# Per-token factors of the RWKV branch made in the projection instead of the chunk loop

## What is computed

```python
z = h @ lp['w_in'][:, :STATE_COLS]
zr = _centred_shift(z[..., 2 * RET_WIDTH:], lp['rwkv_mu'][:, :SHIFT_STATE_COLS])
k, v, wd, ad = _split(zr, (RWKV_WIDTH, RWKV_WIDTH, DECAY_LORA, ICLR_LORA))
kk = kk * lax.rsqrt(jnp.sum(kk * kk, axis=-1, keepdims=True) + 1e-12)
u = lp['rwkv_w0'][:, None, None, :] + jnp.einsum('btr,drc->dbtc', jnp.tanh(wd), lp['rwkv_w2'])
w = jnp.exp(-jnp.exp(-jax.nn.softplus(-u.astype(jnp.float32)) - 0.5))
a = jax.nn.sigmoid(lp['rwkv_a0'][:, None, None, :] + jnp.einsum('btr,drc->dbtc', ad, lp['rwkv_a2']))
k_dir = k[None] * (1.0 + (a - 1.0) * lp['rwkv_k_a'])
# per head and direction, token by token
sa = jnp.einsum('bhvk,bhk->bhv', s, -kkt)
s = (s * wt[:, :, None, :] + sa[..., None] * (kkt * at)[:, :, None, :]
     + vt[..., None] * kt[:, :, None, :])
y = jnp.einsum('bhvk,bhk->bhv', s, xt[5])
bonus = jnp.sum(qu['r'][None] * st['k'] * r_k, axis=-1, keepdims=True).sum(0) * st['v']
```

## Time and profile before

| | us |
|---|---|
| median of the runs | 4059.08 |
| runs | 4056.05, 4059.08, 4069.73 |
| the profiled execution's own time | 4071.43 |
| its span | 4069.6 |
| projection | 0 to about 1184 |
| chunk stage | about 1184 to 2181 |
| TensorE busy over the span | 3694.0 (91%) |
| VectorE, ScalarE, GpSimd busy | 2247.2, 1892.5, 671.5 |

### The profile page before, as it was taken

The page is one execution under the profiler, slowest core; times in us unless marked ns, Lnnn a source line. Parts: engine busy times, 40 slices in busy tenths (PEclk is TensorE's granted clock), DMA queues, the critical chain, the costliest instruction groups (busy, mean ns, idle before and its releaser), DMA issues. The chain is left out here.

```text
span 4069.6 us, 94464 instructions
## 1 busy us (share of the span) xinstructions
PE 3694.0 (91%) x39914; PEld 3087.6 (76%) x39914; DVE 2247.2 (55%) x3650; ACT 1892.5 (47%) x3029; POOL 671.5 (16%) x637
## 2 busy tenths in 40 slices
PE   7999999999978888888887978996699999999993
PEld 6878878888867777777776867785588888888883
DVE  5532533434337777777776865555444544454545
ACT  5533534433336666666565443332244444444443
POOL 1000000000012222222220333200011111111111
PEclk9999999999989999999999989998799999999997
DMA  7655565555442223322324366655366666666667
GB/s 260 199 188 183 179 198 155 154 157 158 149 145 73 69 78 81 81 79 74 96 65 124 111 221 225 202 168 189 134 206 217 214 217 212 214 206 214 212 212 299
DMA packets 378746, 673.49 MB, mean 165 GB/s; under 512 B 90428, under 2 KB 261540, under 8 KB 360712
## 3 DMA queue, kind: packets, MB, share of 16 engines
q1 hardware_dynamic: 351368, 580.69, 44.0%
q0 software_dynamic: 27008, 87.46, 7.4%
HBM read 524.89 MB, written 143.15 MB: 164 GB/s over the span
## 5 line engine op out<-in xcount | busy, mean ns | idle before, releaser
L113 PE MATMUL fro__acc<-fro__hT_hi,fro__wh 128*128 128x512 f32 (+1 forms) x1608 | 624.9, 389 | 11.8 <-DVE fro__hT_lo L2695 8.9
L114 PE MATMUL fro__acc<-fro__hT_hi,fro__wl 128*128 128x512 f32 (+1 forms) x1608 | 612.9, 381 | 0.0
L115 PE MATMUL fro__acc<-fro__hT_lo,fro__wh 128*128 128x512 f32 (+1 forms) x1608 | 612.8, 381 | 0.0
L2112 DVE TENSOR_TENSOR fin__wl<-fin__raw,fin__wh 128x4096 fp32r<-128x4096 f32 x96 | 424.7, 4424 | 316.8 <-ACT fin__wh L2056 316.8
L2701 DVE TENSOR_TENSOR fro__wl<-prj__w,fro__wh 128x1024 fp32r<-128x1024 f32 x201 | 246.3, 1225 | 637.6 <-ACT fro__wh L2484 637.6
L2056 ACT ACTIVATE fin__wh<-fin__raw 128x4096 fp32r<-128x4096 f32 x96 | 348.4, 3629 | 190.8 <-PE exp__acc L115 190.3
L113 PE MATMUL exp__acc<-fin__wh,exp__xh 128*128 128x512 f32 x1024 | 399.9, 390 | 0.8 <-DVE exp__xl L2117 0.8
L115 PE MATMUL exp__acc<-fin__wl,exp__xh 128*128 128x512 f32 x1024 | 398.5, 389 | 0.0
L114 PE MATMUL exp__acc<-fin__wh,exp__xl 128*128 128x512 f32 x1024 | 398.4, 389 | 0.0
L113 PEld LDWEIGHTS fro__acc<-fro__hT_hi,fro__wh 128*128 128x128 f32 x1608 | 303.7, 189 | 77.7 <-issue 22.2
L114 PEld LDWEIGHTS fro__acc<-fro__hT_hi,fro__wl 128*128 128x128 f32 x1608 | 303.8, 189 | 59.1 <-issue 3.6
(11 more groups left out here) (462 smaller groups left out, 7570.1 us busy)
## 6 DMA issues: line engine op xcount, KB each, us to landing
fin__raw<-in_w_x SPq DMA_DIRECT2D x96, 2048.0 KB
prj__w<-in_w_z SPq DMA_DIRECT2D x201, 512.0 KB, 4.1
s_zT<-fro__pool SPq DMA_DIRECT2D x128, 256.0 KB, 4.5
fro__wm<-in_w_mod POOLq DMA_DIRECT2D x16, 1024.0 KB, 5.8
mix__gate<-s_zT SPq DMA_DIRECT2D x64, 256.0 KB, 4.2
prj__xin<-in_tokens SPq DMA_DIRECT2D x18, 512.0 KB, 5.7
rwc__kS<-s_kS SPq DMA_DIRECT2D x36, 256.0 KB, 3.1
rwc__kkn<-s_kkn SPq DMA_DIRECT2D x36, 256.0 KB, 3.3
```

Of the source, the lines that this page charges most:

```text
L113: pe.matmul(out, sh, mh, start=first, stop=False)
L114: pe.matmul(out, sl, mh, start=False, stop=False)
L115: return pe.matmul(out, sh, ml, start=False, stop=last)
L2112: ve.tensor_tensor(wl[s][:, :, :], raw[s][:, :, :], wh[s][:, :, :], ALU.subtract).then_inc(w_lo, 1)
```

## The change

The low-rank products and everything that follows from them per token move from the chunk stage into the projection.

- **Projection.** For each key tile TensorE makes the decay products at five steps after the tile and the rate products at six (`low_rank`: two directions, high part over 128 rows, low part over 64), and in the last block, whose tiles are 513 tokens wide, a group of one-column products at seven. They use `rc` too. ScalarE applies the sigmoids with a bias (`rates`), VectorE makes kd, bb and the bonus product (`unit`) and the low parts (`rests`), GpSimd's queue stores sg, kd, bb and bon for both directions. Its transfers in the projection go from 165 to 317. kS, kka, rrk and waS are no longer written. `zo` has three buffers instead of four. The tiles stand in another order: wa first, keys and queries in pairs.
- **Chunk stage.** Decays, learning, both sigmoids, key1, key2, removal and the bonus product are gone. A load brings sg, bb, kd, kkn, rS and vS, each in three pieces with the upper half swapped, and bon whole: 19 transfers. There are three buffers for them instead of two, and the load for slab h+3 waits, among others, for the bonus matmul of slab h. beta and kappa are one operation each over 128 partitions. The small sums of carried decays go from VectorE to GpSimd.

The diff, cut to its core:

```diff
+    C, HC, NG, GH, LEV, B, LB = P, 64, 2, 4, 5, 4, 3
...
             def load(j):
-                d, c = j % 2, slab_at(j)
-                sp.dma_start(wS[d][0:64, :], T["waS"][0:64, ds(c, C)]).then_inc(lws[d], 16)
-                sp.dma_start(aS[d][0:64, :], T["waS"][64:128, ds(c, C)]).then_inc(lws[d], 16)
-                if j == 0:
-                    low_rank(0)
-                    low_rank_rows(0)
-                    sp.dma_start(scanm[:, :, :], T["scanm"]).then_inc(scan_in, 16)
-                for n in names:
-                    rows = T[n][:, ds(c, C)].rearrange("(q p) t -> p q t", p=P)
-                    if n != "vS":
-                        sp.dma_start(ld[d][n][:, :, :], rows).then_inc(lds[d], 16)
+                u, c = j % LB, slab_at(j)
+                for n in each_way + both_ways:
+                    rows = (T[n][j % 2] if n in each_way else T[n])[:, ds(c, C)].rearrange("(q p) t -> p q t", p=P)
+                    landed = lsg[u] if n == "sg" else lds[u]
+                    if n == "bon":
+                        sp.dma_start(ld[u][n][:, :, :], rows).then_inc(landed, 16)
                         continue
-                    sp.dma_start(ld[d][n][0:HC, :, :], rows[0:HC, :, :]).then_inc(lds[d], 16)
+                    sp.dma_start(ld[u][n][0:HC, :, :], rows[0:HC, :, :]).then_inc(landed, 16)
                     for s in range(2):
-                        sp.dma_start(ld[d][n][HC:P, :, side(s)], rows[HC:P, :, side(1 - s)]).then_inc(lds[d], 16)
+                        sp.dma_start(ld[u][n][HC:P, :, side(s)], rows[HC:P, :, side(1 - s)]).then_inc(landed, 16)
...
             for h in range(SLABS + 3):
-                if h + 2 < SLABS:
-                    for n in ("am", "kd1", "kd2", "bd", "al", "rho", "bonp", "trm"):
+                if h + LB < SLABS:
+                    for n in ("dd2", "betad", "kappad", "al", "rho", "trm", "bonm"):
                         sp.wait_ge(S[n], at(n, h))
-                    load(h + 2)
+                    load(h + LB)
...
+            def carried(j):
+                d = j % 2
+                gp.wait_ge(S["dd"], at("dd", j))
...
+                ways = []
+                for e in range(2):
+                    upto, after = halves(L)[side(e), :, :, 31], halves(D)[side(e), :, :, HC - 1]
+                    enter, leave = (upto, after) if d == 0 else (after, upto)
+                    s, o = turn_of(j, 0) ^ e, turn_of(j, 1) ^ e
+                    gp.tensor_tensor(fl[side(e), 0, :], enter[:, :, s], dl[d][side(e), :], ALU.add)
+                    last = gp.tensor_tensor(fl[side(e), 1, :], enter[:, :, o], leave[:, :, s], ALU.add)
+                    ways.append(leave[:, :, o])
+                last.then_inc(S["fld"], 1)
+                gp.wait_ge(S["fld"], at("fld", j))
+                for e in range(2):
+                    last = gp.tensor_copy(dl[d][side(e), :], ways[e])
+                last.then_inc(S["dld"], 1)
...
+            def scaled_removal(j):
+                ve.wait_ge(lds[j % LB], 16 * NLD * (j // LB + 1) + START)
                 ve.wait_ge(S["ebk"], at("ebk", j))
-                ve.wait_ge(S["bd"], at("bd", j))
                 if j:
                     ve.wait_ge(S["trm"], at("trm", j - 1))
-                tt(beta[0:HC, :, :], bb[0:HC, :, :], e_bk[0:HC, :, :], ALU.mult)
-
-            def scaled(j):
-                ve.wait_ge(S["kd2"], at("kd2", j))
-                for out, rows, signal in ((beta, bb, "betad"), (kappa, kd, "kappad")):
-                    if out is kappa:
-                        tt(out[0:HC, :, :], rows[0:HC, :, :], e_bk[0:HC, :, :], ALU.mult)
-                    for s in range(2):
-                        ins = tt(out[HC:P, :, side(s)], rows[HC:P, :, side(1 - s)], e_bk[HC:P, :, side(1 - s)], ALU.mult)
-                    ins.then_inc(S[signal], 1)
+                tt(beta[:, :, :], ld[j % LB]["bb"][:, :, :], e_bk[:, :, :], ALU.mult).then_inc(S["betad"], 1)
+
+            def scaled_keys(j):
+                tt(kappa[:, :, :], ld[j % LB]["kd"][:, :, :], e_bk[:, :, :], ALU.mult).then_inc(S["kappad"], 1)
...
                     levels(1, h)
                 if prepare:
                     exclusive(n)
-                if prepare:
-                    key1(n)
-                    removal(n)
                 if inverting:
                     levels(2, h)
-                if prepare:
-                    key2(n)
                 if exists(h - 2) and exists(h):
                     state(h - 2, 1)
                 if prepare:
-                    scaled_lower(n)
+                    scaled_removal(n)
                 if inverting:
                     levels(3, h)
                 if prepare:
-                    scaled(n)
-                    carried(n)
...
+            def rates(t, kind):
+                c, p = keys_of[t], ORDER[t][3]
+                j0, end, at = span(t)
+                m = min(end - j0, 512)
+                act.wait_ge(summed, use_of[t, kind] + 1)
+                for x in ((0, 1) if kind == "t" else (int(kind == "a"),)):
+                    out, stored = (sg, av)[x], (sg_out, bb_out)[x]
+                    for d in range(2):
+                        if kind == "t":
+                            ins = act.activation(out[d][:, 512:513], rc[:, x, d:d + 1], ACT.Sigmoid, bias=low_b[:, x, d, p:p + 1])
+                            continue
+                        if c:
+                            act.wait_ge(stored[d], 16 * c)
+                        ins = act.activation(out[d][:, 0:m], rc[:, d, 0:m], ACT.Sigmoid, bias=low_b[:, x, d, p:p + 1])
+                ins.then_inc(read, 1)
...
+            def low_rank(t, kind):
+                p = ORDER[t][3]
+                j0, end, at = span(t)
+                m = min(even(end - j0), 512)
+                pe.wait_ge(low_ok, 3)
+                pe.wait_ge(rank_in, 32 * (ORDER[t][0] + 1))
+                pe.wait_ge(read, use_of[t, kind])
+                for x in ((0, 1) if kind == "t" else (int(kind == "a"),)):
+                    own = slice(64 * x, 64 * x + 64)
+                    for d in range(2):
+                        hi, lo, mov = low_hi[:, x, d, p * P:(p + 1) * P], low_lo[own, d, p * P:(p + 1) * P], rank[x]
+                        if kind == "t":
+                            out = rc[:, x, d:d + 1]
+                            pe.matmul(out, hi.bitcast(F32), mov[:, 512:513].bitcast(F32), start=True, stop=False)
+                            mm = pe.matmul(out, lo.bitcast(F32), mov[own, 512:513].bitcast(F32), start=False, stop=True)
+                            continue
+                        pe.matmul(rc[:, d, 0:m], hi, mov[:, 0:m], start=True, stop=False)
+                        mm = pe.matmul(rc[:, d, 0:m], lo, mov[own, 0:m], start=False, stop=True)
+                mm.then_inc(summed, 1)
...
+                for x, kind in enumerate("wat"):
+                    if s - 5 - x in keys_of and (s - 5 - x, kind) in use_of:
+                        low_rank(s - 5 - x, kind)
...
+            def unit(t, d, i, held):
...
+                ve.tensor_scalar(kd, rate, -1.0, par[:, 1, p:p + 1], ALU.add, ALU.mult).then_inc(kd_half, 1)
+                ve.wait_ge(kd_half, i + 1)
+                ve.scalar_tensor_tensor(kd, kd, 1.0, XY[moved_of[t] % 4][:, 1, 1 + j0:1 + end], ALU.add, ALU.mult).then_inc(kd_ok, 1)
+                ve.wait_ge(kkn_ok, c + 1)
+                ve.scalar_tensor_tensor(rate, rate, -1.0, kkn[c % 2][:, 0:n], ALU.mult, ALU.mult).then_inc(bb_ok, 1)
+                if b:
+                    r = moved_of[query_at[b, p]]
+                    ve.wait_ge(kd_ok, i + 1)
+                    ve.wait_ge(shifted, r + 1)
+                    if held:
+                        ve.wait_ge(kb_out[1], 16 * held)
+                    ve.scalar_tensor_tensor(kb[1][:, 0:n], kd, par[:, 2, p:p + 1], XY[r % 4][:, 1, 1 + j0:1 + end], ALU.mult, ALU.mult).then_inc(bon_ok, 1)
...
 def tile_order():
 
 
-    ctx = [(Z_K + p, "k", p, ACT.Copy) for p in range(4)] + [(Z_WA, "wa", 0, ACT.Copy)] + [(Z_V + p, "v", p, ACT.Copy) for p in range(4)]
+    keys, vals, quer = [[(z + p, n, p, ACT.Copy) for p in range(4)] for z, n in ((Z_K, "k"), (Z_V, "v"), (Z_R, "r"))]
+    ctx = [(Z_WA, "wa", 0, ACT.Copy)] + [t for pair in zip(keys, vals) for t in pair]
     plain = [(Z_RK + p, "z", 0, ACT.Copy) for p in range(8)]
     first = [ctx[i // 2] if i % 2 == 0 else plain[i // 2] for i in range(17)]
-    turned = ctx[0:4] + [ctx[5], ctx[4], (Z_GD, "gd", 0, ACT.Copy)] + ctx[6:9] + [(Z_R + p, "r", p, ACT.Copy) for p in range(4)]
+    turned = ctx[0:1] + [t for pair in zip(keys, quer) for t in pair] + [(Z_GD, "gd", 0, ACT.Copy)] + vals
...
+SCRATCH = {"mod_rows": [2, MOD], "zT": [NZ * P, TOK], "sg": [2, HALF, TOK], "bb": [2, HALF, TOK], "kd": [2, HALF, TOK],
+           "bon": [2, HALF, TOK], "kkn": [HALF, TOK], "vS": [HALF, TOK], "rS": [HALF, TOK], "gT": [HALF, LAT], "y": [2, TOK, HALF], "bonus": [2, P, TOK],
```

376 lines of the change are left out of this document (182 added, 194 removed).

## The result

The changed kernel takes 4256.81 us (median of 4 runs, 4251.48 to 4261.30) against 4060.96 us of the kernel before: a ratio of 1.0479, 95% interval 1.0457 to 1.0502. It is slower, as forecast, but by 196 us where 106 were forecast, and 4256.81 lies outside the range of 4070 to 4250. The profiled execution took 4251.48 us, span 4249.6; the kernel before had 4071.43 and 4069.6, so the two traces differ by 180.0 us.

The account below looks back on a forecast made before the run. TensorE bounds the latent projection, a chain between engines the chunk loop, closed after the change by SP's issues. Projection +55, loops +64, last loops -13 make +106 on 4071.43: 4177 us profiled, 4165 by the median; range 4070 to 4250.

Parts of the forecast that it names:

- The mechanism: Chunk stage: SP's longer load issue delays y's stores, ScalarE waits for yo; loop 29.0 us, +64 us in 30 loops.
- Rival A: Chunk stage: SP does not close the loop, so the whole 4.3 us come out; 3959 us; chance 0.14.
- B: Chunk stage: SP closes the loop but the clock stays up, 26.8 us a loop; 4099 us; chance 0.18.
- C: Chunk stage: y lands later than 2.8 us behind many small packets; 4249 us if doubled; chance 0.12.
- D: Whole kernel: gains and losses cancel, within 0.3% of before; chance 0.05.
- a load is 12.3 us: Chunk stage, SP's queue: 18 pieces at 0.65 us plus one whole tensor at 0.6 make 12.3 us.
- the clock costs 2.2 us: Chunk stage: a half-speed stretch after TensorE's long idle costs 2.2 us a loop, ends 1.2 and 2.5.
- gain of 4.3 us a loop: Chunk stage: removing the mask wait, decay and learning products and a table load shortens the chain by about 4.3 us.
- a low-rank product costs its pitch, 0.227: Projection, TensorE: a 512-column matmul costs 0.227 us, so the low-rank products of sixteen latent key tiles cost 29.1 us.
- My own sign: Projection: TensorE full yet the stage ending over 80 us later would mean missed waits on the shared bank.
- The context block: Projection's context block: four key tiles' work on nearly full VectorE and ScalarE adds 8 us, ends 0 to 15.
- The start: Start of chunk stage: shorter VectorE key work set against longer first loads, nothing net, -15 to +15 us.

Follow-up runs that it names:

- e1: Changed kernel with the two stores of y issued ahead of the load on SP: 4056.22 us, ratio 0.9961 to the kernel before.
- e3: Changed kernel with every load tensor brought by one transfer, 7 issues instead of 19 (wrong halves, time only): 4047.68 us, loop 24.06 us.
- e4: Changed kernel with the same 19 load pieces, upper-half rows of 512 bytes instead of 256 (wrong data, time only): 4253.56 us.

## Why the prediction was wrong, point by point

- **The mechanism was right and is shown.** SP's issue list closes the loop through the y stores and the one yo buffer; the wait stands where I put it, and moving four lines (e1) or cutting the issues (e3) takes it away. Rival A, SP does not bind, fell with the trace (its counter-argument, "no issue in the trace is under 0.48 us", holds for the loop shown and not for the trace, where some of other tensors take 0.25 and 0.33); B fell with the clock of 0.86; C fell with e4, rows of 512 bytes change nothing, and y landed in 2.1 us, quicker than my 2.8; D fell with the 196 us. ScalarE's wait is longer than the 4 to 5 us that I named, 7.0 in the mean.
- **The step "a load is 12.3 us" was mis-sized.** I took 6.06 us for the ten issues from one loop. Over 32 loads of the kernel before the mean was 6.65, and 6.06 was the shortest; some issues take 0.5 to 1.4 us longer than the others (that of kka 0.56 in the median, 1.99 at most). Of nineteen issues more of them are hit: 14.8 us in the mean, 0.78 an issue instead of 0.65. The loop came to 30.5 for 29.0: 2.5 more from the load and 0.2 from the stores, less 0.6 from y's quicker landing and 0.6 from the stretch behind the wait. Times 30 these are the 45 us that the loops were over.
- **The step "the clock costs 2.2 us"** held: 2.0 to 2.1 measured, and its mechanism too, an idle stretch and then 0.50. The stretch that it is added to was taken too long, 9.4 us for 8.9 to 9.0 at the full clock.
- **The gain of 4.3 us a loop** was somewhat too large. Once nothing waits for SP the loop is 23.61 us against 26.87, 3.3 less. Behind slab 33 only two loops end in a bonus copy, and they gave 2.9 us each, 5.8 together, where I had counted three at 4.3.
- **The step "a low-rank product costs its pitch, 0.227"** failed. I took the pitch of equal operands for a group in which 64 and 128 rows alternate; it is 0.42. Instead of 1.03 us (four products and the start) a group costs 1.72, 32 x 0.7 = 22 us too little. With a range of 42 to 80 for the projection I had bounded waits on the bank, not this. My own sign, "over 80 us later, the shared bank's waits are what I have missed", pointed the wrong way: it came at 85 us, and in the latent blocks TensorE never waits.
- **The context block** was taken at 8 us with 0 to 15; all but the products it is 12 to 14 (the run without them is 12.2 us late at the first latent step and 14.3 at the next), near the upper end. A part of it is the clock, which I had looked for in the chunk stage alone, and 5.4 us are two waits on the shared bank. The one-column groups were right as products, 2.4 us for 8, where I took 2.2; that the clock falls behind some of them, some 3 us in all, stood nowhere in the sum.
- **The start** gave 3.1 us, and the stages behind the chunk stage 5.6 us, within what one execution differs from the next as far as these runs show; nothing in the change touches them.
- **The range** ended at 4250 although the ends of its terms, 80 for the projection and 130 for the loops, less 13, add to 197 and reach 4256. A range narrower than that supposes that the errors do not lie on the same side; here both did and added to 75 us. With the mean of the loads (6.65 for 6.06) in place of the shortest, the forecast would have been some 35 us higher.

## What to carry to other kernels

When a queue that issues transfers also carries stores which something waits for, count its list in issues and not in bytes, with the mean of an issue over many loops, and put the stores ahead of the loads. A gain on the engines is worth what the list leaves of it: here 4.3 us a loop became a loss of 3.7, and four moved lines turned the loss into a gain of 3.3. And price an added matmul from rows whose neighbours have its own operand shapes.

## What the runs showed of the hardware that I had not expected

- Each change between products of 128 and of 64 rows costs 0.2 us at 512 columns: 1.61 us for a group of four that alternate, 1.20 for high, high, low, low, 0.92 when all have 128 rows. Behind a change the weight load starts with its product and not one pitch ahead of it.
- An issue on SP costs 0.65 us in the median for a piece of 64 partitions, 64 or 128 KB, and 0.55 for 256 KB over 128 partitions behind another of its kind (0.65 for bon, which stands behind a piece); rows of 256 or 512 bytes make no difference (14.80 and 14.82 us a load). Nineteen pieces cost 14.8 us where seven whole transfers of the same bytes cost 4.9.
- Filling part of an idle stretch of TensorE with idle products keeps the clock up in some loops and only moves its fall in others: with gaps of 0 to 2.4 us left it stayed at 1.00 in 18 of 28 loops, and behind a gap of 2.9 us it was 0.59 over the next 3 us.
- The clock can fall while TensorE has work without a break: it was 0.50 from 1132 to 1135 us, behind 2.4 us of one-column products.
